# Hybrid decoder layer on one core: tile 0 finished ahead at the end of phase one, 24 gather steps in phase one at a closer pace

## What is computed

```python
h = rms_norm(x); z = h @ w_in            # q, k, v (1536 each), conv GLU 2048, gates 2048
A = silu(layer_norm(depthwise_conv(glu(z), 31))) @ w_conv_proj
B = dilated_attention(q, k, v) @ w_attn_proj        # 3 groups x 8 heads x 64; the sample reads caches
x1 = x + (sig(gA) * A + sig(gB) * B) @ w_out
h2 = rms_norm(x1); s = (h2 @ w_peer_q) . sub_keys   # 8 heads x 2 halves x 128 keys
idx, g = top 16 of the sums of two top-16 lists     # per token and head: 128 experts
y = x1 + sum_k g_k * gelu(h2 . expert_u[idx_k]) * expert_v[idx_k]
```

## Time and profile before

| | |
|---|---|
| median of 3 runs | 2151.61 us (2147.18 to 2158.86) |
| profiled execution | 2151.05 us, span 2149.1 us |
| TensorE busy | 1597.1 us, 74% |
| VectorE busy | 1374.1 us, 64% |
| ScalarE busy | 825.1 us, 38% |
| GpSimd busy | 793.7 us, 37% |
| DMA | 745.14 MB, mean 347 GB/s |

### The profile page before, as it was taken

How to read it: one execution, slowest core, us unless ns; L and a number is a source line. 1 busy time by engine, 2 the same in 40 slices (tenths; PEclk the granted TensorE clock), 3 DMA queues, 4 the chain that set the end, 5 groups by cost and what they waited for, 6 DMA issues and landing times.

```text
span 2149.1 us, 33388 instructions
## 1 busy us (share of the span) xinstructions
PE 1597.1 (74%) x11692; PEld 729.1 (34%) x11692; DVE 1374.1 (64%) x3347; ACT 825.1 (38%) x2404; POOL 793.7 (37%) x713
## 2 busy tenths in 40 slices
PE   7989999898998997777778988895444445444444
PEld 3556655444444443434433433341100001110000
DVE  1477655123468788967766666447767767777774
ACT  2133333201545535544546533334433333433332
POOL 1255100001323354444532322344555554455553
PEclk9999999999999999999989999997555556655555
DMA  5433466837999999999999999999999999999998
GB/s 186 150 115 115 174 221 237 312 138 246 384 414 386 385 372 422 375 364 385 360 393 378 389 417 410 401 418 394 421 421 421 419 413 403 416 418 416 421 412 345
DMA packets 125794, 745.14 MB, mean 347 GB/s; under 512 B 15892, under 2 KB 39052, under 8 KB 47916
## 3 DMA queue, kind: packets, MB, share of 16 engines
q0 software_dynamic: 78336, 570.46, 65.6%
q1 hardware_dynamic: 47292, 172.55, 21.5%
HBM read 727.36 MB, written 16.44 MB: 346 GB/s over the span
## 4 chain that ended last, share of the span: by engine, by line
PE 36%; DMA 26%; DVE 20%; issue 7%; ACT 4%; POOL 2%; SPq 0%; DVEq 0%; POOLq 0%; ACTq 0%; PEldq 0%
DMA ring<-in_expert_uv,pick 24%; PE z L1210 20%; DVE ring L1990 7%; PE acc L1382 5%; PE z L1216 1%; PE s L1235 1%; DVE ti L1873 1%; ACT fold L1555 1%; DMA ring<-in_v_cache 1%; DVE ti L1876 1%; POOL ring L1139 1%; DVE tv L1875 1%; PE o L1245 1%; PE s L1512 1%; ACT gel L1552 1%
## 5 line engine op out<-in xcount | busy, mean ns | idle before, releaser
L1139 POOL DMA_INDIRECT ring<-in_expert_uv,pick x544 | 662.1, 1217 | 874.5 <-PE acc L1382 806.2
L1990 DVE CUSTOM_DVE_ANT_0 ring<-ring,rep 128x1024 f32<-128x1024 f32 x544 | 664.8, 1226 | 405.0 <-DMA ring<-in_expert_uv,pick 356.9
L1382 PE MATMUL acc<-ring,fold 128*32 128x256 f32 x4352 | 455.1, 505 | 451.5 <-ACT fold L1555 451.0
L1210 PE MATMUL z<-wts,hT 128*128 128x384 f32 (+1 forms) x1408 | 599.8, 563 | 4.1 <-DMA wts<-in_w_glu 2.4
L1382 PEld LDWEIGHTS acc<-ring,fold 128*32 128x32 f32 x4352 | 104.0, 124 | 774.7 <-ACT fold L1555 712.7
L1210 PEld LDWEIGHTS z<-wts,hT 128*128 128x128 f32 x1408 | 255.4, 195 | 251.0 <-issue 181.0
L1552 ACT ACTIVATE gel<-dots 128x1 f32<-128x1 f32 x544 | 108.6, 200 | 594.6 <-DVE dots L1990 593.4
L1210 PE MATMUL z<-wts,yT 128*128 128x512 f32 x384 | 184.4, 615 | 3.0 <-ACT yT L1570 1.6
L1555 ACT ACTIVATE fold<-by_pick,gel 128x32 f32<-128x32 f32 x544 | 174.8, 321 | 18.1
L1548 ACT ACTIVATE by_pick<-cst,pick 128x32 f32<-128x32 f32 x544 | 167.3, 308 | 0.0
L1865 DVE SCALAR_TENSOR_TENSOR yT<-uT,vec,yT 128x256 f32<-128x256 f32 x240 | 106.0, 496 | 2.0
(11 more groups left out here) (291 smaller groups left out, 1688.6 us busy)
## 6 DMA issues: line engine op xcount, KB each, us to landing
wts<-in_w_qkv SPq DMA_DIRECT2D x24, 1536.0 KB, 8.1
wts<-in_w_glu SPq DMA_DIRECT2D x8, 2048.0 KB, 12.7
wts<-in_w_gate SPq DMA_DIRECT2D x8, 2048.0 KB, 11.9
wts<-in_w_wq SPq DMA_DIRECT2D x8, 2048.0 KB, 11.6
ring<-in_k_cache SPq DMA_DIRECT2D x16, 768.0 KB, 7.9
ring<-in_v_cache SPq DMA_DIRECT2D x16, 768.0 KB, 7.4
ring<-in_expert_uv,pick POOLq DMA_INDIRECT x544, 11.3
wts<-in_w_cp SPq DMA_DIRECT2D x4, 2048.0 KB, 11.7
```

What stands on the lines that cost most here:

```text
L1139: eng.indirect_dma_start(ring[:, i % RING, :], None, a["expert_uv"], bass.IndirectOffsetOnAxis(picks(i, 0).bitcast(U32), 0)).then_inc(row_ ...
L1210: mm = eng.matmul(bank[:, 0:w], of[:, k, :], rows[:, k, :], start=(k == 0), stop=(k == depth - 1))
L1382: mm = eng.matmul(acc[b][SUB * c:SUB * (c + 1), col:col + 256], fold[:, i % 4, :], ring[:, i % RING, D + 256 * c:D + 256 * (c + 1)], start ...
L1990: eng.tensor_tensor_reduce(u, u, rep[:, j, :], 1.0, 0.0, ALU.mult, ALU.add, dots[:, i % 4:i % 4 + 1]).then_inc(dot_ready, 1)
```

## The change

- Ahead of the other two tiles, tile 0 goes through the products at the end of phase one: cp 1, ap 0 and ap 1 of tile 0 come first, then cp 1 of the others, wo 0 and wo 1 of tile 0, ap of the others, wq 0 of tile 0, wo of the others, and so on. wq 2 and wq 3 keep their order. By the new list wq 0 of tile 0 takes ticks 36 to 39 (47 to 50 before), `START` is tick 47 (58), the gap tick is gone and phase two begins at tick 82 (83). (DV, 0, 1), (DV, 1, 1) and what follows them are two ticks later: (DV, 1, 1) at tick 16, (DH, 1) at tick 19.
- For that, more weight units must be in the memory at a time. ap 0, ap 1 and wo 1 are loaded into ring slots 3, 4 and (2, 5), the latter in two loads of 1 MB. ap 0 and ap 1 wait for (DT, 1, 1), wo 1 for (DV, 1, 1), (DH, 1) and the sample's stores. The other units take turns in the two places of `wts`. The first gather into slot 3, 4, 2 or 5 waits for the last use of what lies there.
- Phase one holds up to 24 steps, one each 2.6 of planned cost instead of 3.2. 248 steps are left for phase two, 272 for the tail.

```diff
-            again = max(first + 23, conv_last + 6)
+            again = max(first + 25, conv_last + 6)
...
+        if p == 0:
+            units += [("cp", 0, 1), ("ap", 0, 0), ("ap", 0, 1), ("wo", 0, 0), ("wo", 0, 1), ("wq", 0, 0), ("wq", 0, 1)]
+            late = [("cp", 0, 1), ("ap", 0, 0), ("ap", 0, 1), ("cp", 1, 1), ("cp", NT, 1), ("wo", 0, 0), ("wo", 0, 1), ("ap", 1, 0), ("ap", 1, 1), ("ap", NT, 0), ("ap", NT, 1),
+                    ("wq", 0, 0), ("wo", 1, 0), ("wo", NT, 0), ("wo", 1, 1), ("wo", NT, 1), ("wq", 0, 1), ("wq", 1, 0), ("wq", NT, 0), ("wq", 1, 1), ("wq", NT, 1)]
+        for kind, t, j in late:
...
+            if (kind, t, j) == ("wq", 0, 0):
+                now = max(now, ends["wo", 0, 1] + 6)
+            e = use(t, kind, j)
+            after[kind](t, j, e)
+        if p == 0:
+            inputs(2, now)
...
+IN_RING = {UNIT_NO["ap", 0, 0]: (3,), UNIT_NO["ap", 0, 1]: (4,), UNIT_NO["wo", 0, 1]: (2, 5)}
...
-        marks[n] = min(16, int(early[n - START - 7] / 3.2))
+        marks[n] = min(24, int(early[n - START - 7] / 2.6))
...
-                if u >= 2:
-                    eng.wait_ge(z_ready, last_use(u - 2) + 1)
+                if u in IN_RING:
+                    eng.wait_ge(tp_ready, TB.no["DT", 1, 1] + 1)
+                elif WTS_BEFORE[u] is not None:
+                    eng.wait_ge(z_ready, last_use(WTS_BEFORE[u]) + 1)
...
+                for x, r in enumerate(IN_RING[u]):
+                    if r < 3:
+                        eng.wait_ge(k_used, 8)
+                    elif r == 5:
+                        eng.wait_ge(tp_ready, TB.no["DH", 1] + 1)
+                        eng.wait_ge(d_out, 16 * HP * NG)
+                    eng.dma_start(ring[:, r, :], a["w_" + kind][n][:, 2 * D * x:2 * D * (x + 1)]).then_inc(w_ring_in[u], 16)
...
+                    if i in RING_NEEDS:
+                        eng.wait_ge(z_ready, RING_NEEDS[i])
                     eng.indirect_dma_start(ring[:, i % RING, :], None, a["expert_uv"], bass.IndirectOffsetOnAxis(picks(i, 0).bitcast(U32), 0)).then_inc(row_in[i % RING], 16)
```

More of the change, by code:

```diff
@@ L249, in inputs, with behind_cp, behind_ap, behind_wo @@
         put(at + 3, ("XT", t, 1))
+    def behind_cp(t, half, e):
+        put(e + 1, ("c", t, half))
+    def behind_ap(t, half, e):
+        put(e + 1, ("a", t, half))
+        put(e + 2, ("MT", t, half))
+    def behind_wo(t, j, e):
+        put(e + 1, ("w", t, j))
+        if j == 0:
+            return
+        put(e + 2, ("N0", t))
+        s = 2 if t == NT else 0
+        if t == NT:
+            put(e + 3, ("ND", t))
+            put(e + 4, ("NP", t))
+        put(e + 3 + s, ("N1", t))
+        put(e + 4 + s, ("ro", t))
+        put(e + 4 + s, ("HT", t, 0))
+        put(e + 5 + s, ("HT", t, 1))
+    def behind_wq(t, j, e):
+        put(e + 1, ("k", t, j))
+        put(e + 2, ("QT", t, j))
+        put(e + 4, ("SC", t, j))
+        put(e + 5, ("so", t, j))
+    after = {"cp": behind_cp, "ap": behind_ap, "wo": behind_wo, "wq": behind_wq}
     for p in range(2):
@@ L333, in plan @@
         ends["late", p] = max(now, last) + 2
-        for half in range(2):
+        for half in range(2 if p else 1):
             for t, e in each(p, "cp", half):
-                put(e + 1, ("c", t, half))
-        for half in range(2):
+                behind_cp(t, half, e)
+        late = []
+        if p == 0:
+            units += [("cp", 0, 1), ("ap", 0, 0), ("ap", 0, 1), ("wo", 0, 0), ("wo", 0, 1), ("wq", 0, 0), ("wq", 0, 1)]
+            late = [("cp", 0, 1), ("ap", 0, 0), ("ap", 0, 1), ("cp", 1, 1), ("cp", NT, 1), ("wo", 0, 0), ("wo", 0, 1), ("ap", 1, 0), ("ap", 1, 1), ("ap", NT, 0), ("ap", NT, 1),
+                    ("wq", 0, 0), ("wo", 1, 0), ("wo", NT, 0), ("wo", 1, 1), ("wo", NT, 1), ("wq", 0, 1), ("wq", 1, 0), ("wq", NT, 0), ("wq", 1, 1), ("wq", NT, 1)]
@@ L338, in plan @@
+        for kind, t, j in late:
+            if kind == "rest":
+                now += 1
+                continue
+            if (kind, t, j) == ("wq", 0, 0):
[4 more added lines that the diff above has]
+            inputs(2, now)
+        for half in range(2 if p else 0):
             for t, e in each(p, "ap", half):
-                put(e + 1, ("a", t, half))
-                put(e + 2, ("MT", t, half))
+                after["ap"](t, half, e)
@@ L341, in plan @@
         assert p or again + 21 < ends["ap", NT, 0]
[L342 to L356, removed]
@@ L357, in plan @@
-        now = ends["wo", PAIRS[p][0], 1] + 6
-        for j in range(4):
-            for t, e in each(p, "wq", j):
[L360 to L365, removed]
+        if p:
+            now += 1
+            for j in range(2):
+                for t, e in each(p, "wo", j):
+                    after["wo"](t, j, e)
+            now = ends["wo", PAIRS[p][0], 1] + 6
@@ L366, in plan @@
+        for j in range(0 if p else 2, 4):
+            for t, e in each(p, "wq", j):
+                after["wq"](t, j, e)
+            if p == 0 and j == 2:
+                inputs(3, now)
         ends["conv", p] = (conv_first, conv_last)
@@ L392, with weight_homes @@
 QK_NO = {s: e for e, s in enumerate(QK)}
+IN_RING = {UNIT_NO["ap", 0, 0]: (3,), UNIT_NO["ap", 0, 1]: (4,), UNIT_NO["wo", 0, 1]: (2, 5)}
+WTS_SLOT, WTS_BEFORE, WTS_LOAD = {}, {}, {}
+def weight_homes():
+    last, count = [None, None], [0, 0]
+    for u in range(len(UNITS)):
+        if u not in IN_RING:
+            s = sum(count) % 2
+            WTS_SLOT[u], WTS_BEFORE[u], WTS_LOAD[u] = s, last[s], count[s]
+            last[s], count[s] = u, count[s] + 1
+weight_homes()
 def unit_of(u):
@@ L402, in last_use, with tick_of @@
     return USE_NO[(s[0], PAIRS[s[1]][-1], *s[2:])]
+def tick_of(task):
+    return next(n for n, some in enumerate(TICKS) if task in some)
+RING_FROM = {u: tick_of(("DT", 1, 1)) if max(rs) < 5 and min(rs) > 2 else tick_of(("DH", 1)) if max(rs) == 5 else tick_of(("DV", 1, 1)) for u, rs in IN_RING.items()}
+RING_NEEDS = {r: max(USE_NO[(UNITS[u][0], NT, *UNITS[u][2:])] + 1 for u, rs in IN_RING.items() if r in rs) for r in sorted({r for rs in IN_RING.values() for r in rs})}
 def tick_phase(n):
@@ L964, in _ @@
             for n, tick in enumerate(TICKS):
-                while loaded < len(UNITS) and ENDS[USES[last_use(loaded - 2)]] < n:
+                while loaded < len(UNITS) and (RING_FROM[loaded] if loaded in IN_RING else ENDS[USES[last_use(WTS_BEFORE[loaded])]]) < n:
                     load(loaded)
@@ L1182, in use_begins @@
                 n = unit_of(u)
-                eng.wait_ge(w_in[n % 2], 16 * (n // 2 + 1))
+                if n in IN_RING:
+                    eng.wait_ge(w_ring_in[n], 16 * len(IN_RING[n]))
+                else:
+                    eng.wait_ge(w_in[WTS_SLOT[n]], 16 * (WTS_LOAD[n] + 1))
                 bank_free(eng, ZB, z_free, u)
```

25 lines of the change are left out of this document (16 added, 9 removed).

## The result

The changed kernel is slower: median 2169.37 us against 2151.61. Two of its five executions took 3868 and 5849 us and are left out of the ratio to the kernel before, which is 1.0067 with a 95% interval of 1.0047 to 1.0086. The profiled execution took 2166.14 us (before 2151.05), 15.1 us more. From here on I cut each trace at three marks: the first matmul of cp in phase one, phase two's first matmul, and the end of phase two's last weight product.

What follows compares the result with a forecast made beforehand. It took DMA to bound the tail and most of phase two. TensorE's path (+14.2 - 16.3 = -2.1 us) and DMA's account (about -9) led to -6 us: 2145.0 profiled, 2145.5 median, range 2127 to 2167.

Steps and rivals of the forecast that it cites:

- rival 2: Phase one's dense stretch: rows come too late, TensorE stands 21 us, time 2170; decides from about 2.9 us a step; chance 0.16.
- What bounds the kernel: Tail set by DMA alone, phase two mostly by DMA; only filling DMA idle time ahead of the tail gains.
- The start of the gathers: Phase one: START 11 ticks earlier, terms summing to 16.8 us, taken as 14 to 15; first gather at 510, not 524.18.
- rival 3: The gathers' start doesn't move, because the last value portion or wo 1 comes late; 0 to +3 us, 2152; chance 0.13.
- The value portion: Phase one, (DV, 1, 1): the last value portion queues behind more weights; net wait +4.0 us, bounds -3.85 and +7.9.
- GpSimd's stand before gather 2 and the late norm: Phase one: GpSimd stands 2 to 5 us, tile 1's norm power follows four gathers; +2.3 us, bounds 0 and +5.
- Waits for folds: those of the 16 steps now are small; +1 us: Phase one: TensorE's added waits for the folds of the steps, put at +1 us, with rival 2 as upper bound.
- DMA share over 0.95 from 515 us on: Sign to look for: DMA engines stay fed from 515 us on, even through phase one's last ten ticks without steps.
- my +14.2: Sum of the phase one terms: phase two's first matmul moves 14.2 us later, from 597.33 to 611.5 us.
- wq 2 and the third head's scores: Late phase one: +1 us for wq 2's load (bounds 0, +11), +1 us for tile 0's third head's scores (0, +8).
- Phase two -16.3 us: Phase two with 248 steps instead of 256: 2.1 at 0.64 us, 5.9 at 2.54; bounds -5.1 and -20.3.
- The two sums: Whole kernel: TensorE's path gave -2.1 us, DMA's account about -9 by filling 9.3 us of idle time; -6 was taken.

Runs made afterwards that it cites:

- e4: The kernel before with 16 steps moved from phase two to the tail; median 2160.90 us, ratio 1.0029 to the kernel before.
- e2: The kernel before, in its old order, with 23 steps at pace 2.6 in phase one; median 2164.79 us, ratio 1.0046 to the kernel before.
- e5: The changed kernel with its 24 steps at pace 3.7 and wo 0 loaded after the last value portion; median 2151.27 us, ratio 0.9986 to the kernel before.
- e7: The changed kernel, wo 0 after the values, gathers 2 to 5 after tile 1's norm power, first step at START + 4, 28 steps at 3.6; 2129.22 us.
- e10: As e7, but with 24 steps at pace 4.1 in phase one; median 2145.52 us, ratio 0.9956 to the kernel before.
- e14: e7 with the step marks of e10 in phase two, phase one unchanged; median 2141.55 us, ratio 0.9940 to the kernel before.
- e15: e10 with the step marks of e7 in phase two, phase one unchanged; median 2131.75 us, ratio 0.9894 to the kernel before.
- e9: As e7, but with the first step at START + 7 and 28 steps at pace 3.2; median 2132.91 us, ratio 0.9898 to the kernel before.

## Why the prediction was wrong

I forecast 2145.5 us and no clear change. The time is that of rival 2 (2170), to which I gave 0.16, but in part by luck: its mechanism, rows too late in the dense stretch, is there at half its size (9.7 us of waits more, not 21, under the 15 that I had set as its sign), and a phase two shorter by 6.7 us instead of 16.3 made up for the rest; that is under the 8 us at which I had called the forecast wrong. Step by step:

- **What bounds the kernel: right.** The tail lasts as long as before and moves 411 GB/s. The Trainium skill's limit of about 358 GB/s for one core ("DMA: Bandwidth & Descriptors", Specifications) is not borne out here either.
- **The start of the gathers: right, better than forecast.** 505.11 us instead of 510; rival 3 fell. Counted from cp's begin it is 16.9 us earlier, my unrounded sum of 16.8; the other 2.2 are cp's own, which I hadn't forecast (it begins at 387.25, 386.55 and 385.80 us in before, e4 and e2, alike up to there, so part of it is what executions differ by). SC of tile 0 ended at 490.7 (496 forecast), and P waited 0.93 us for the search. But the search's load on VectorE showed elsewhere: an eviction behind it made TensorE wait 3.63 us, so 4.56 together, as the 4.76 of the earlier trace rows.
- **The value portion: right.** The wait grew from 3.85 to 6.87 us (forecast +4.0, measured +3.0). e5 shows that the order in the queue makes it: 1.6 us once the weights are issued behind it. That agrees with the Trainium skill, "DMA: Bandwidth & Descriptors", Queues, rings and completion order, by which a DMA engine takes a queue's descriptors in ring order. I had not priced the slow clock behind it, 2.4 us.
- **GpSimd's stand before gather 2 and the late norm: the place right.** The stand was 0.85 us, not 2 to 5, but the norm still waited 2.61 us (2.3 forecast), since its power came behind the gathers.
- **"Waits for folds: those of the 16 steps now are small; +1 us": this step failed.** They went from 3.8 to 13.5 us, +9.7. Steps 0 to 23 ran from 529.33 to 600.8 us, 71.5/23 = 3.1 us each, over the 2.9 from which I said that rival 2 decides. Against that rival I had put six gathers in flight 20 us before the first fold. The lead was there and was worth six steps, no more: with the ring full GpSimd stood 12.85 us, and the DMA engines lost 3.4 + 2.7 = 6.1 us in 520 to 540, of the 9.3 us that the earlier start was to fill. "DMA share over 0.95 from 515 us on" was wrong for this reason, and again at 610 us (0.51), where I had argued that six gathers and two weight units would keep them fed.
- **The granted clock: not priced.** Some 6.1 us of slower matmuls behind waits. With the folds' 8.7 us beyond forecast this is 14.8, against 12.1 us by which phase one exceeded my +14.2; the search, the value portion, wq 2 and the scores came out some 5 us under their terms.
- **wq 2 and the third head's scores: no harm.** Neither shows a wait in phase one, where I had 1 us each.
- **"Phase two -16.3 us": the price right, the sum wrong.** e4 measured 2.19 us a step, 17.5 for eight, between my bounds of 5.1 and 20.3. But only 6.7 us came, 10.8 are missing, and the DMA engines stand idle 10.1 us more in phase two than before (19.9 against 9.8). The largest hole is behind the knot that the new marks tied on VectorE: 0.07 + 0.62 of 10 us, 6.9 us from 690 to 710 us. I treated steps as amounts and did not ask where the marks put the searches. That it is the marks is shown on e7 and e10, by e14 and e15; for the changed kernel itself it is argued from the same rows.
- **The two sums.** Averaging the TensorE path (-2.1) and the DMA account (-9) was no safe middle: each assumed that the other side hid its losses, and the kernel paid both. The DMA account was the right book with a wrong entry: idle time didn't fall by 9.3 us, it grew by 4.1 in phase one and by 10.1 in phase two.

## What to carry to other kernels

An earlier start of a ring is worth its slots and no more; unless the first consumption moves with it, the idle time only comes a little later (what moving it is worth could not be told from e7 and e9). Spread extra steps at a pace that DMA can serve (here at 2.6 of planned cost 3.1 us were taken for each, at 3.6, with the first step three ticks nearer, the engines stayed full) and up to the end of the stage. When a change shifts counters by which other work is placed, list what now shares a tick: the same number of steps in other places made 12 to 14 us here, nearly as much as the whole change cost.

## What the runs showed of the hardware

A wait of TensorE can cost more than itself. After 6.07 us without work four matmuls took 3.78 us instead of 1.98, the granted clock's lower level (1.2 instead of 2.4 GHz); after 6.87 us the 32 matmuls of (DV, 1, 1) took 6.01 instead of 3.64. A short wait is no safe case: after 3.85 us in the earlier trace rows they still took 3.64, but in e4, the same program up to there, the same wait was followed by
```profile
427.54 6.17 PE L1298 MATMUL o<-ring,rep 128*32 128x512 f32 x32 [3.87 <-DMA ring<-in_v_cache]
```
which makes 2.5 of the 3 us by which e4's phase one is longer: the clock is part of what executions of one program differ by.

A crowded 10 us on VectorE (9.26 busy) showed as 115 GB/s of DMA 20 us later, with full queues of gathers between: the engine that is late and the engine that stands idle are far apart in time.
